# A one-core encoder step: expert blocks add their rows into the output in place, and experts are paired e with e+32

## What is computed

```python
x = x + gate1 * mix
h = rmsnorm(x, norm2_w) * (1 + scale2) + shift2
x = x + gate2 * hierarchical_moe(h, ...)

# hierarchical_moe, cut
g_w, g_idx = lax.top_k(softmax(h @ w_router_group + b), 1)       # 1 of 8 groups
e_w, e_idx = lax.top_k(softmax(e_logits_of_that_group), 2)       # 2 of its 8 experts
expert_id = g_idx * 8 + e_idx
combine_w = g_w * e_w / sum(e_w)
y_e = (silu(x @ w_gate[e]) * (x @ w_up[e])) @ w_down[e]          # D_EXPERT = 512
y[token] += combine_w * y_e                                      # over the token's two experts
```

## Time and profile before

| what | us |
|---|---|
| median of 3 runs | 1814.07 |
| lowest and highest | 1812.19, 1815.24 |
| span of the profiled execution, first to last instruction | 1811.6 |
| PE busy in that span | 1470.8 (81%) |
| DVE, ACT, POOL busy | 398.0, 269.1, 333.5 |
| share of the span in the chain that ended last: PE 43%, DMA 43%, DVE 7% | |

### The profile page before, as it was taken

The page is one execution under the profiler, slowest core; times in us unless marked ns, Lnnn a source line. Parts: engine busy times, 40 slices in busy tenths (PEclk is TensorE's granted clock), DMA queues, the critical chain, the costliest instruction groups (busy, mean ns, idle before and its releaser), DMA issues.

```text
span 1811.6 us, 21590 instructions
## 1 busy us (share of the span) xinstructions
PE 1470.8 (81%) x8206; PEld 836.3 (46%) x8207; DVE 398.0 (22%) x884; ACT 269.1 (15%) x544; POOL 333.5 (18%) x522
## 2 busy tenths in 40 slices
PE   3679999999999999299977878787777777799972
PEld 2678888788889745233322222222222222233320
DVE  1633433442442232611010101010101010011104
ACT  2312312323231212001000000000000000001001
POOL 2453434344241000101101010101010010101110
PEclk8787898799789998599999999999999999999996
DMA  9451331232130544097999999999999999866995
GB/s 324 129 150 49 99 104 52 87 110 92 54 109 24 194 145 165 8 379 324 420 420 420 421 421 420 421 421 420 420 420 420 420 417 411 355 270 281 420 421 210
DMA packets 135826, 491.27 MB, mean 271 GB/s; under 512 B 14188, under 2 KB 66188, under 8 KB 86108
## 3 DMA queue, kind: packets, MB, share of 16 engines
q1 hardware_dynamic: 119648, 468.21, 64.6%
q0 software_dynamic: 12624, 13.57, 2.4%
q10 hardware_dynamic: 3532, 9.21, 1.6%
HBM read 495.86 MB, written 25.50 MB: 288 GB/s over the span
## 4 chain that ended last, share of the span: by engine, by line
PE 43%; DMA 43%; DVE 7%; ACT 3%; issue 3%; SPq 1%; ACTq 0%; POOL 0%; DVEq 0%; POOLq 0%
DMA ws<-in_w_down 39%; PE ps L664 13%; PE ps L880 8%; PE ps L869 6%; PE ps L789 4%; PE ps L726 3%; PE ps L757 3%; ACT arena L1000 2%; DVE arena L1183 2%; DMA ws<-in_w_in 1%; PE ps L744 1%; DMA ws<-in_w_up 1%; PE ps L809 1%; PE ps L627 1%; DVE small L1206 1%
## 5 line engine op out<-in xcount | busy, mean ns | idle before, releaser
L869 PE MATMUL ps<-ws,arena 128*64 128x512 f32 x2240 | 519.4, 612 | 139.1 <-DMA ws<-in_w_gate 79.5
L869 PEld LDWEIGHTS ps<-ws,arena 128*64 128x64 f32 x2240 | 160.9, 140 | 495.5 <-issue 322.6
L664 PE MATMUL ps<-ws_r 128*128 128x274 f32 x1600 | 300.4, 308 | 9.7 <-issue 9.7
L880 PE MATMUL ps<-ws,arena 128*64 128x512 f32 x1120 | 253.8, 598 | 45.4 <-DVE arena L1397 30.3
L664 PEld LDWEIGHTS ps<-ws_r 128*128 128x128 f32 x1600 | 250.7, 205 | 16.4 <-issue 15.1
L376 POOL TENSOR_TENSOR held<-small 128x1 f32<-128x1 f32 x195 | 38.6, 201 | 1086.6 <-ACT arena L1082 631.4
L664 PE MATMUL ps<-arena_r,ws_r 128*128 128x274 f32 x800 | 176.9, 305 | 0.0
L880 PEld LDWEIGHTS ps<-ws,arena 128*64 128x64 f32 x1120 | 75.2, 136 | 199.8 <-issue 124.6
L1394 DVE TENSOR_TENSOR arena<-arena,ps 128x512 f32<-128x512 f32 x35 | 24.1, 688 | 632.8 <-PE ps L869 632.8
L664 PEld LDWEIGHTS ps<-arena_r,ws_r 128*128 128x128 f32 x800 | 137.0, 204 | 0.0
L507 POOL TENSOR_TENSOR ws_r<-ws,ws_r 128x1024 fp32r<-128x1024 f32 x48 | 117.5, 2449 | 3.8
(11 more groups left out here) (254 smaller groups left out, 1123.8 us busy)
## 6 DMA issues: line engine op xcount, KB each, us to landing
ws<-in_w_gate SPq DMA_DIRECT2D x64, 2048.0 KB, 26.7
ws<-in_w_down SPq DMA_DIRECT2D x64, 2048.0 KB, 26.5
ws<-in_w_up SPq DMA_DIRECT2D x64, 2048.0 KB, 26.9
ws<-in_w_ada SPq DMA_DIRECT2D x12, 2048.0 KB, 8.8
ws<-in_w_in SPq DMA_DIRECT2D x48, 512.0 KB, 3.8
ws<-yc_dram SPq DMA_DIRECT2D x4, 1024.0 KB, 8.1
merged<-in_x_prompt SPq DMA_DIRECT2D x4, 512.0 KB, 5.7
biasq_dram<-bias_dram POOLq DMA_DIRECT2D x1, 2048.0 KB, 16.3
```

The source lines that it names most:

```text
L664: last = nc.tensor.matmul(ps[:, 2 * buf + h, 0:HALF], w[:, k, :], x[:, k, HALF * h:HALF * h + HALF], start=(k == 0 and part == 0), stop=(k ...
L869: last = nc.tensor.matmul(ps[CAP * e:CAP * e + CAP, m, :], xT[:, 4 * c + k, CAP * e:CAP * e + CAP], w[:, e, k, :], start=(c == 0 and k == ...
L880: last = nc.tensor.matmul(ps[CAP * e:CAP * e + CAP, 4 + h, :], hTm[:, 2 * c + k, CAP * e:CAP * e + CAP], w[:, e, k, 512 * h:512 * h + 512] ...
```

## The change

The expert stage no longer writes rows to a buffer that is combined at the end. Each block reads the present output rows of its tokens, adds its contribution, and writes them back.

- As soon as `x1` (the residual) is there, SP stores it to `y_p` and `y_s`. The reload, the combination on ACT and DVE and the final stores are gone, and so is `yc_dram`.
- For each block POOL first gathers `prev`, the present output rows of the block's tokens: one indirect DMA from `y_p` with the token numbers in `toki`, and, when it has landed, one from `y_s` with `srow`, which has a number in range for the rows of sample tokens alone. Then comes the gather of block `blk + 2`'s input rows, as before. Behind `y_dve` it issues two scatters, to `y_p` and to `y_s`, and waits for both.
- DVE makes `gmix`, the gate row times the weight of each row of the block (two operations of 128 x 1024), multiplies both PSUM banks by it into `yb`, waits for `prev` and adds it. ACT no longer evacuates half of the result.
- The slot matmuls (line 836) carry 96 columns in place of 48, the row's weight beside its number. DVE makes `blkw` ahead of them, and `wpr` and `srow` behind them.
- Pair q consists of experts q and q + 32. A token's two experts are of one group of eight, so no block holds a token twice. Experts 5, 53 and 54 now lie in pairs 5, 21 and 22, which again gives 35 blocks.

```diff
@@ views
-        wg2 = g["w_gate"][0].rearrange("(q e) (p k) n -> q p e (k n)", e=2, p=P)
+        wg2 = g["w_gate"][0].rearrange("(e q) (p k) n -> q p e (k n)", e=2, p=P)
...
@@ SP
+            for t, (_, rows, _) in enumerate(TILES):
+                sp.wait_ge(x1_rdy, t + 1)
+                sp.dma_start(y_rows[t], x1[0:rows, t, :]).then_inc(x1_st, 16)
             sp.wait_ge(oinfo_rdy, 1)
...
-            stored = sp.value_load(oinfo[0:1, O_ST:O_ST + 1], min_val=16, max_val=16 * NBLK)
-            sp.wait_ge(y_st, stored)
-            for t, (_, rows, _) in enumerate(TILES):
-                sp.dma_start(ws[0:rows, t, 0:2 * D],
-                             yc_dram[2 * P * t:2 * P * t + 2 * rows, :].rearrange("(p c) n -> p (c n)", c=2)).then_inc(yc_ld[t], 16)
-            for t, (_, rows, _) in enumerate(TILES):
-                sp.wait_ge(fin_rdy, t + 1)
-                sp.dma_start(y_rows[t], ws[0:rows, t, 0:D]).then_inc(out_st, 16)
...
@@ POOL
             def gather_and_scatter(i, blk, u):
 
+                ch(pool.tensor_copy(cur[:, 2:3], toki[:, bass.ds(blk, 1)]))
+                hold(nc.gpsimd)
+                pool.indirect_dma_start(out=prev, out_offset=None, in_=y_p[0], in_offset=row_of(2),
+                                        bounds_check=SEQ - 1, oob_is_err=False).then_inc(prev_ld, 16)
+                ch(pool.tensor_copy(cur[:, 3:4], srow[:, bass.ds(blk, 1)]))
+                pool.wait_ge(prev_ld, 32 * blk + 16)
+                hold(nc.gpsimd)
+                pool.indirect_dma_start(out=prev, out_offset=None, in_=y_s[0], in_offset=row_of(3),
+                                        bounds_check=DEC - 1, oob_is_err=False).then_inc(prev_ld, 16)
                 pool.wait_ge(mxT_mm, blk + 1)
                 pool.wait_ge(xg_ld[u], 16 * i + 16)
...
                 gather(blk + AHEAD, u)
-                ch(pool.tensor_copy(cur[:, 2:3], dsti[:, bass.ds(blk, 1)]))
-                pool.wait_ge(y_act, blk + 1)
                 pool.wait_ge(y_dve, blk + 1)
                 hold(nc.gpsimd)
-                pool.indirect_dma_start(
-                    out=yc_dram, out_offset=bass.IndirectOffsetOnAxis(ap=cur[:, 2:3], axis=0),
-                    in_=yb[:, u, :], in_offset=None,
-                    bounds_check=2 * NTOK - 1, oob_is_err=False).then_inc(y_st, 16)
-                pool.wait_ge(y_st, 16 * blk + 16)
+                pool.indirect_dma_start(out=y_p[0], out_offset=row_of(2), in_=yb[:, u, :], in_offset=None,
+                                        bounds_check=SEQ - 1, oob_is_err=False).then_inc(y_st, 16)
+                pool.indirect_dma_start(out=y_s[0], out_offset=row_of(3), in_=yb[:, u, :], in_offset=None,
+                                        bounds_check=DEC - 1, oob_is_err=False).then_inc(y_st, 16)
+                pool.wait_ge(y_st, 32 * blk + 32)
                 hold(nc.gpsimd).then_inc(y_free, 1)
...
@@ ACT, the copy of g2bc and the end
-                    n = P if s == 0 else DEC
+                    n = P if s == 0 or part == 5 else DEC
...
-                act.wait_ge(slot_used[5], blk + 1)
-                act.wait_ge(y_dve, blk + 1)
-                nc.scalar.activation(yb[:, u, 0:512], ps[:, 4, :], ACT.Copy).then_inc(y_act, 1)
...
@@ DVE
+            ch(V.tensor_tensor(blkw, blkhot, column(wts.rearrange("p t c -> p (t c)"), NBLK), ALU.mult))
             V.tensor_tensor(blkhot, blkhot, column(val, NBLK), ALU.mult).then_inc(dest_rdy, 1)
...
-            V.tensor_copy(dsti[:, 0:NBLK], stab).then_inc(table_rdy, 1)
-            dve.wait_ge(table_rdy, 1)
-            V.tensor_scalar(toki[:, :], dsti[:, :], 1, None, ALU.logical_shift_right).then_inc(table_rdy, 1)
+            V.tensor_copy(toki[:, 0:NBLK], stab).then_inc(table_rdy, 2)
+            ofp = over[:, 0:NBLK]
+            ch(V.tensor_scalar(ofp, stab, float(SEQ), None, ALU.is_lt))
+            ch(V.tensor_tensor(wpr[:, 0, :], ofp, ps[:, 7, NBLK:2 * NBLK], ALU.mult))
+            ch(V.tensor_tensor(wpr[:, 1, :], ps[:, 7, NBLK:2 * NBLK], wpr[:, 0, :], ALU.subtract))
+            ch(V.scalar_tensor_tensor(out=ofp, in0=ofp, scalar=OOB, in1=stab, op0=ALU.mult, op1=ALU.add))
+            V.tensor_scalar(srow[:, :], ofp, -float(SEQ), None, ALU.add).then_inc(wslot_rdy, 1)
...
+                ch(V.tensor_scalar(gmix, g2bc[:, 0, :], wpr[:, 0, bass.ds(blk, 1)], None, ALU.mult))
+                ch(V.scalar_tensor_tensor(out=gmix, in0=g2bc[:, 1, :], scalar=wpr[:, 1, bass.ds(blk, 1)], in1=gmix,
+                                          op0=ALU.mult, op1=ALU.add))
                 dve.wait_ge(y_free, blk + 1)
                 dve.wait_ge(slot_used[5], blk + 1)
-                V.tensor_copy(yb[:, u, 512:D], ps[:, 5, :]).then_inc(y_dve, 1)
+                ch(V.tensor_tensor(yb[:, u, :].rearrange("p (h n) -> p h n", h=2), ps[:, 4:6, :],
+                                   gmix.rearrange("p (h n) -> p h n", h=2), ALU.mult))
+                dve.wait_ge(prev_ld, 32 * blk + 32)
+                V.tensor_tensor(yb[:, u, :], yb[:, u, :], prev, ALU.add).then_inc(y_dve, 1)
```

More of the change, by code:

```diff
@@ L139, in encoder_step @@
         cur = sb("cur", [P, 4], U32)
-        oinfo = sb("oinfo", [1, O_ST + 1], I32)
+        oinfo = sb("oinfo", [1, O_N], I32)
         wts = sb("wts", [P, NTT, 2])
+        wpr = sb("wpr", [P, 2, NBLK])
         ARENA = 20640
@@ L266, in encoder_step @@
         hTm = region(o + 8 * D, DE).rearrange("p (k n) -> p k n", k=4)
+        prev = region(o + 9 * D, D)
+        gmix = region(o + 10 * D, D)
         ssq, rstd, ssq2, rstd2 = small[:, 0:5], small[:, 5:10], small[:, 10:15], small[:, 15:20]
@@ L324, in encoder_step @@
         router_ld = sem("router_ld")
-        yc_ld = [sem(f"yc_ld{i}") for i in range(NTT)]
+        prev_ld, x1_st = sem("prev_ld"), sem("x1_st")
         biasrow_st, ada_st = sem("biasrow_st"), sem("ada_st")
@@ L362, in encoder_step @@
         silu_rdy, hm_rdy, hTm_mm, hTm_rdy = (sem(n) for n in ("silu_rdy", "hm_rdy", "hTm_mm", "hTm_rdy"))
[L363 to L364 removed]
+        y_dve, wslot_rdy = sem("y_dve"), sem("wslot_rdy")
         act_ch, dve_ch, pool_ch = sem("act_ch"), sem("dve_ch"), sem("pool_ch")
@@ L835, in _ @@
                     i = 2 * t + c
-                    last = nc.tensor.matmul(ps[:, 7, 0:NBLK], rowhot[0:rows, i, :], blkhot[0:rows, i, :],
+                    last = nc.tensor.matmul(ps[:, 7, 0:2 * NBLK], rowhot[0:rows, i, :], slotrhs[0:rows, i, :],
                                             start=(i == 0), stop=(i == 2 * NTT - 1))
@@ L1096, in _ @@
                         hidden(2 * i + (NPAIR + 1), 1)
-            for t, (_, rows, _) in enumerate(TILES):
-                act.wait_ge(yc_ld[t], 16)
-                nc.scalar.activation(ws[0:rows, t, 0:D], ws[0:rows, t, 0:D], ACT.Copy,
-                                     scale=wts[0:rows, t, 0:1]).then_inc(t0_rdy, 1)
         @block.vector
         def _(dve):
-            ch, ch2 = Chain(dve, dve_ch), Chain(dve, fin_ch)
+            ch = Chain(dve, dve_ch)
             V = nc.vector
@@ L1417, in _ @@
                         hidden(2 * i + (NPAIR + 1), 1)
-            for t, (_, rows, s) in enumerate(TILES):
-                y0, y1 = ws[0:rows, t, 0:D], ws[0:rows, t, D:2 * D]
-                dve.wait_ge(t0_rdy, t + 1)
-                ch2(V.scalar_tensor_tensor(out=y0, in0=y1, scalar=wts[0:rows, t, 1:2], in1=y0, op0=ALU.mult, op1=ALU.add))
-                ch2(V.tensor_tensor(y0, y0, g2bc[0:rows, s, :], ALU.mult))
-                V.tensor_tensor(y0, y0, x1[0:rows, t, :], ALU.add).then_inc(fin_rdy, 1)
 def bucket_onehot():
```

39 lines of the change are left out of this document (22 added, 17 removed).

## The result

The changed kernel takes 1835.9 us (median of 4, 1833.7 to 1837.5) against 1814.7 for the kernel before (median of 4, 1812.2 to 1815.4): a ratio of 1.0132, 95% interval 1.0106 to 1.0157. It is slower, by 21 us. The profiled execution has a span of 1833.4 us, 21.8 more than before.

The account below looks back on a forecast made before the run. The prediction took weight loads to bound the expert stage. Its terms, -24.4 (end), +41.6 (stream of transfers) and +0.5 (routing), summed to +17.7 us, so 1829.3, or 1832 as the median, with 8 in 10 from 1812 to 1850.

Parts of the forecast that it names:

- The bound: Expert stage: bound by loads of weights, 4.97 us each, six taking 29.8 us of a 31.00 us period.
- The price of an indirect DMA: Beside the weight loads: each indirect DMA of 128 rows costs 0.33 us whatever it carries, bounds 0.25 and 0.39.
- The clue that it set aside: Expert stage: the engines' mean rate stays near 420 GB/s, which hides that a landing waits for the slowest engine.
- The stream: Expert blocks: three more indirect DMAs and prev's rows cost 1.3 us a block, 41.6 us over 32 blocks.
- The expert distance: Weight loads: experts 32 apart instead of adjacent in one load change nothing, as pieces keep their size; 0 us.
- Rival (a): Expert blocks: skipped rows cost next to nothing, 0 to 0.1 us a DMA beside its bytes; 1800 to 1810 us; chance 0.12.
- Rival (b): Expert blocks: POOL's chain of landings becomes the bound, deciding from 32.3 us; at 34, 1865 to 1875 us; chance 0.09.
- Rival (c): Whole kernel: gain and cost cancel, with 0.22 us an indirect DMA and a dry spell less; 1811 to 1817 us; chance 0.06.
- the prediction's bound for the order of blocks: Expert blocks: double pairs move to other places in the order; taken as 0 us, bounds -2 to +3.
- The tail: End of the kernel: from PE's last matmul 7.9 us instead of 32.35, a gain of 24.4 us if prev is in time.
- The routing: Before the expert blocks: blkw, 48 more columns and small operations cost +0.5 us, bounds -1 to +2.
- DVE and ACT at 0: Inside a block: DVE's added operations and ACT's lost evacuation cost 0; PE doesn't notice prev late by under about 11 us.

Follow-up runs that it names:

- the four kernels: The kernel before (median 1811.9 to 1812.8 us), and that kernel with only its rows spread (1797.2), only the new pairs (1818.9), only its rows crowded (1835.1).
- chain shortened: The changed kernel without the gather from and the scatter to the sample output; 1833.8 us, ratio 1.0118.
- loads relieved: The changed kernel with each block's rows permuted so that they spread over the partitions; 1819.4 us, ratio 1.0048.
- both -21 (998.7): The changed kernel with rows spread, POOL's short loop and one output buffer, so one gather and one scatter for outputs a block; 1806.4 us, ratio 0.9976.
- the reordered kernel: The changed kernel with the gather of input rows for block b+2 issued ahead of the two gathers of prev; 1883.4 us, ratio 1.0429.

## Why the prediction was right in its number and wrong in its terms

- **The bound** (weights; 4.97 us a load; 29.8 of 31.0 us) held: with the rows spread the periods shown are 30.2 us, and the line through the four kernels meets no rows at all at 29.8.
- **The price of an indirect DMA**, 0.33 us each, is the step that failed. It divided the 0.7 us left over after "bytes at the mean rate" by the number of DMAs; a DMA without rows costs 0.07. But the rows' own share was the one that was too small: not 0.5 us by 16 engines, but four rows on one engine, 1.24 us. The last lines of the prediction name the case, a cost that isn't the same for each DMA, and the DMA from `y_s`. The clue that it set aside ("the mean hides that a landing waits for the slowest engine") was right, too, and pointed at the rows. And the 0.1 us a DMA that it kept for a rival lay near the measured 0.07.
- **The stream**, +41.6, measured +33.9. In its place: pairing +6.0, `prev` +26.2, the two sample DMAs, which is to say POOL's chain, +1.7. By the rows on the busiest engine `prev` makes 173 x 0.155 = 27 us, and the pairing 12 rows x 2 x 0.155 = 3.7 of its 6.0; the rest of that isn't settled. The expert distance was costed at 0 because the pieces are of one size; it changes which tokens share a block.
- **Rival (a)** has a lesson of its own. Its condition came true, skipped rows cost 0.07 us, less than the 0.15 from which it was to decide. Its time, 1800 to 1810, didn't, since it too took the rows at the mean rate. The Trainium skill's rule that it named ("DMA: Bandwidth & Descriptors", section "Anatomy of one DMA") agrees with these runs in that a DMA without rows takes next to nothing from the stream; its bytes over the full rate are too little for a DMA whose rows lie on a few engines.
- **Rival (b)**, POOL's chain, came true in its mechanism but not in its cost. 31 us were predicted for a turn, and the one shown has 31.05, with 10.65 for the two scatters where 11 was taken. The step that failed is its condition, that it decides from 32.3 us on. That compared one period with one turn. Over the whole loop the stream alone asks for 29.9 us a block (1017.9 over 34), since the blocks of 23.3 us are among them, and the chain for 30.1, and it never caught up behind the short blocks. The sign given for (b) shows in part: DVE waits for `prev` in 34 blocks, but PE waits for the input rows and not for `hh_`. It costs nearly nothing, because two limits of almost equal length hide each other: chain shortened -1.7, loads relieved -14, both -21 (998.7). The period of 32.3 that was predicted is 31.8 in the mean of the 26 that aren't near 23.3.
- **Rival (c)**, 1811 to 1817, doesn't follow from its own terms: 0.22 us a DMA give +6.8 us with the other terms as they are, 1821, and the prediction's bound for the order of blocks takes 2 off that.
- **The tail**, 7.9, measured 24.0, is the mis-sized term: 3.6 us from `prev` that came late, since its chain began when the scatters before it had landed beside the last loads (DVE was ready at 1810.7 and added at 1814.4), 0.7 less for the steps behind it, and 13.2 of skipped turns and drain on POOL, which stood hidden in the kernel before and in no view of it. The steps of the prediction ended at the landing; this program ended with POOL's drain.
- **The routing**, +0.5, measured +0.7. DVE and ACT at 0: that holds as long as DVE isn't kept by a late `prev` from the product that PE needs next; in the reordered kernel PE waits 184.8 us for it.

## What to carry to other kernels

When a gather or scatter moves only some of its rows beside a stream of loads, count the rows on the busiest DMA engine, not the DMAs and not the bytes: spreading the live rows over the partitions gave this kernel 15 us, for one changed constant. Where two limits lie close together, compare what each asks for over the whole loop, not one period with one turn. Take apart a leftover like "0.7 us for two DMAs" by an experiment before it is multiplied by 96. And if work is removed from the end of a program, look at what the other engines still do there.

## What was not expected of the hardware

- A turn of POOL's loop that only tests a flag takes 1.04 us in the changed kernel and 1.2 in the kernel before. POOL's drain at the end takes 5.7 to 6.0 us in the kernels with five indirect DMAs a block, the kernel before with three skipped ones among them, and 8.8 to 9.0 in those with two or three. Why isn't settled.
- 128 skipped rows cost the stream 0.07 us, and 0.99 us of POOL's time to issue.
- The indirect DMAs of the changed kernel land after 7.7 to 9.3 us in the median; both ends of that are DMAs with nearly all rows skipped (lines 579 and 591). The shortest, beside few loads, have 2.1 to 3.1. So a chain of four landings is some 31 us beside the loads even where they move little.
- The trace doesn't name the engine of a packet. That the partitions of one group share an engine is the Trainium skill's rule ("DMA: Bandwidth & Descriptors", section "The descriptor swizzle"); the runs show that the time follows it in both directions and in size (1797, 1812, 1835). Whether it is the engine or something else that such a group of partitions shares, and whether a gather and a scatter cost the same, they don't tell.
